# A two-layer hybrid attention step on one core: output products moved beside the last attention units, and three smaller moves

## The chip, the cores and the metric

The kernel runs on one NeuronCore of a Trainium2 chip. The metric is the device time of one execution in microseconds (us). A difference of 0.2%, about 2.8 us here, is about what a measurement of this kernel can tell from no change.

The engines are called as in the profile: PE is the matrix engine (PEld its weight loads), DVE the vector engine, ACT the scalar engine, POOL the general engine, SP the queue engine that issues most transfers. Each runs its own list of instructions in order; they are tied together by semaphores alone.

## What is computed

There are 384 tokens in three tiles of 128: tile 0 is the prompt, tiles 1 and 2 are the sample. The model width D is 2048. Two layers run one after the other.

```
x = x + gate * ((o * silu(g)) @ w_out)      per layer, o = attention over heads of width 128
layer 0: 8 heads of kind A (grouped query), 8 heads of kind B (neighbourhood, with a bias)
layer 1: 16 latent-attention heads; keys and values are made from a compressed state
y = rmsnorm(x) * final_norm                 after layer 1
```

In front of each layer stand a norm and a modulation; `q @ k`, softmax and `p @ v` are done per head and token tile. Prompt queries see 128 keys, sample queries 384.

## The kernel before, in words

**Weights and slots.** All weight matrices stream from HBM in pieces of 512 KB, the slots: two blocks of 128 rows by 512 columns. A chunk of 512 output columns takes eight slots (`SPC = 8`). Products are made in three matmuls from rounded parts: ACT copies the raw slot into `w_hi` (`split_hi`), DVE writes the remainder into `w_lo` (`split_lo`, L1176). Both are issued two slots ahead. The left operand is likewise held as `act_hi` and `act_lo`. `chunk_slot` on PE runs one slot for all three token tiles: 3 tiles x 2 blocks x 3 matmuls, into the banks `G[0..2]`.

**Attention units.** A unit is one head and one token tile. PE does four things for unit n: it turns its probabilities (`prob_turn`), computes the scores of unit n+2, does `attend` of unit n-1, and then runs one slot of some following product where `beside(n)` gives one. DVE does, per unit, `prob_copy`, `maximum` of unit n+2, `output` of unit n-1 (this writes the gated result into `u`), and then any `split_lo`. ACT does the exponentials. `attend` of a unit waits for `output` of the unit before it (`o_done`). Groups A0, A1 and B0 have 12 units each, with a product beside them. The last group of layer 0, B1 (12 units), and the last pair of heads of layer 1 (6 units) have none.

**Output product.** `turned_chunk` begins after the last `output`. It turns `u` block by block on PE (16 blocks of 128 columns, three transposes each, into the banks `BX`), ACT copies each into `act_hi`, DVE makes `act_lo`. Four blocks are turned ahead of the first slot, the others two behind each slot.

**Gates.** The last chunk before a group's units is its gate. ACT evacuates each gate tile twice (a half and a tanh, `evacuate_gate`): tile 0 ahead of the `split_hi` of the last slot, tiles 1 and 2 behind the exponential of unit 2. DVE finishes all three tiles at unit 1 (`finish_gate`, L1347).

**Queries of group A.** The four heads of a group are turned behind slots 4 to 7 of the gate chunk (`turn_in`), the first waiting for `qn_ready`, and DVE copies them into `qT`.

**Behind layer 0.** POOL waits for the last `output` and then loads gains, gate rows (through HBM, `gate_rows`), and the residual input. DVE's `residual(0)` (L1384, L1388) waits for these. The remainders of slots ten and eleven of the output product stand behind it on DVE.

**End.** After each tile's last residual, DVE sums squares, POOL takes the power, ACT scales the left half of the token's 2048 columns, DVE the right half, and SP stores two halves per tile (L386, L388). POOL waits for all stores (`y_out`) and leaves; a barrier of all engines ends the program (L168).

Of the kernel before, what the change touches and what calls it, by code (L numbers as in the profile page):

```python
# [54 lines left out]
N_A, N_B, N_OUT, N_GATE, N_H = 2, 2, D // CH, D // CH, 4  # L55
LAST = 3
Y_CUT = D // 2
# [108 lines left out]
def build(nc, t_in, t_out):  # L166
    ctx = ExitStack()
    with ctx:  # L168
# [160 lines left out]

        def evac_of(pair, c):  # L330

            return pair + ((0, None, 1, None, 2, 3, 4, 5)[c])
# [3 lines left out]
        def _(sp):  # L336
# [46 lines left out]
            for t in range(NT):  # L383
                out = t_out["y_prompt"][0] if t == 0 else t_out["y_sample"][0, (t - 1) * P:t * P, :]
                sp.wait_ge(y_left, t + 1)
                sp.dma_start(out[:, 0:Y_CUT], u[:, t, 0:Y_CUT]).then_inc(y_out, 16)  # L386
                sp.wait_ge(y_right, 2 * t + 2)
                sp.dma_start(out[:, Y_CUT:D], u[:, t, Y_CUT:D]).then_inc(y_out, 16)  # L388


        @block.tensor
        def _(pe):
# [17 lines left out]
            def chunk_slot(w, j, m, made=None, banks=G, depth=NT):  # L410
# [5 lines left out]
                for t in range(NT):  # L416
# [13 lines left out]
                last.then_inc(w_used, 1)  # L430
# [118 lines left out]
            def turn_out(x, parts, width=P, height=P):  # L549
                need(pe, x_free, x + 1 - len(BX))  # L550
                turn(BX[x % len(BX)], parts, width, height).then_inc(x_done, 1)
# [8 lines left out]
            def turned_chunk(x, w, m, made):  # L560

                for k in range(2 * KPS):
                    turn_out((x + k), token_blocks(u, k * P))
                for j in range(SPC):
                    chunk_slot((w + j), j, m, made)
                    for k in range(KPS * (j + 2), min(KPS * (j + 3), KT)):
                        turn_out((x + k), token_blocks(u, k * P))
# [67 lines left out]
            for i in range(N_A):  # L635
                m, tau, n0 = (M_A + i * (2 * NT)), (T_A + i * T_A_PER), (N_UA + i * UNITS)
                for j in range(SPC):
# [4 lines left out]
                    chunk_slot((W_A + j + i * (2 * SPC)), j, m)  # L642
# [26 lines left out]
            for i in range(N_B):  # L669
                w0, m = W_B + i * 4 * SPC, (M_B + i * 4 * NT)  # L670
                tau, n0 = (T_B + i * T_B_PER), (N_UB + i * UNITS)
                for j in range(3 * SPC):
                    if j == 3 * SPC - 1:
                        need(pe, t_free, tau + 2 * GROUP)
                        score(n0, 0, 0, 0)
# [8 lines left out]
                    if SPC + 1 <= j < SPC + 5:  # L684
# [4 lines left out]
                        turn_in(tau + (GROUP + h), [b[0], kcache[:, h * P:(h + 1) * P], b[1], b[2]])  # L689
                pe.wait_ge(vc_in, 16 * (i + 1))  # L690
# [6 lines left out]
                for n in range(UNITS):  # L697
# [5 lines left out]
                    for j in beside(n) if i < N_B - 1 else []:  # L703
                        chunk_slot((w0 + 3 * SPC + j), j, m + (3 * NT))
# [41 lines left out]
            def pair_product(g, c):  # L746
# [16 lines left out]
                bank_ = PAIR_BANKS[c % 4]  # L763
                if c < 4:
# [30 lines left out]
            def pair_attention(g, following):  # L795

                for n in range(PAIR_UNITS):
# [30 lines left out]
            pe.wait_ge(o_done, N_UH + N_H * UNITS)  # L828
            pe.wait_ge(t_free, T_H + N_H * T_H_PER)
            turned_chunk(X_U1, W_O1, M_O1, (x_free, X_U1))  # L830
# [7 lines left out]
        def _(act):  # L838
# [27 lines left out]
            def turned_high(x, out, width):  # L866

                need(act, x_done, x + 1)
                copy(out, BX[x % len(BX)][:, 0:width]).then_inc(xhi, 1)
# [80 lines left out]
            for i in range(N_A):  # L950
                m, tau, n0 = (M_A + i * (2 * NT)), (T_A + i * T_A_PER), (N_UA + i * UNITS)
                for j in range(SPC):
# [16 lines left out]
                    if j == SPC - 1:  # L969
                        exponent(n0, 0)  # L970
                        exponent(n0 + 1, 1)
                        need(act, qn_ready, (NT + i * NT))
                        evacuate_gate(m, w, i * CH, [0])
                    split_hi(w + 2)
                exponent(n0 + 2, 2)
                evacuate_gate(m, (W_A + SPC - 1 + i * (2 * SPC)), i * CH, [1, 2])
# [972 lines left out]
```

## Time and profile before

| | |
|---|---|
| time, median of 3 runs | 1412.71 us (1412.57 to 1413.67) |
| the profiled execution | 1412.55 us |
| its span, first to last instruction | 1410.8 us |
| mean granted PE clock | 0.995 of full |
| busy share | PE 96%, PEld 75%, DVE 43%, ACT 35%, POOL 4% |
| chain that ended last | PE 91%, DVE 4%, DMA 2%, issue 2%, ACT 1% |

The span lies 1.75 us under the execution's own time. A row of the timeline gives the start, the duration, the engine, the line, the operation, output and inputs, and in square brackets how long the engine was idle before it and what released it. Matmuls overlap: what one costs in a stream is the distance from start to start. A 32-bit score, transposition or `attend` is two passes, so "x2" can be one matmul of the code.

### The profile page before, as it was taken

The numbers are of one execution on the slowest core, as the hardware profiler recorded it, in microseconds if no ns is written. First come the engines' busy times: TensorE is split into PE (matmuls) and PEld (weight loads), VectorE is DVE, ScalarE is ACT, GpSimd is POOL, SyncE is SP. The second block draws the span as 40 slices with busy tenths as digits, with TensorE's granted clock in tenths as the row PEclk, the third lists the DMA queues.
The fourth block names the chain that finished last, engine by engine and source line by source line (L and its number), as shares of the span: only waits on it lengthen the run. The fifth ranks groups of instructions, "written<-read, shape, count | busy, mean of one in ns | idle before, by whom it ended". The sixth has DMA issues, their size and how long they took to land.

```text
span 1410.8 us, 17524 instructions
## 1 busy us (share of the span) xinstructions
PE 1359.5 (96%) x7011; PEld 1062.4 (75%) x7011; DVE 613.3 (43%) x1018; ACT 487.6 (35%) x806; POOL 61.6 (4%) x81
## 2 busy tenths in 40 slices
PE   6999999999999999999999899999999999999995
PEld 2567667677777777767888788888888998878884
DVE  3345644553332642236544532533434444445444
ACT  4234233232222322233334653333433333334332
POOL 3000000000100010001000100000000000010000
PEclk9999999999999999999999999999999999999998
DMA  9998767767767357743455343443322222134552
GB/s 370 395 404 337 279 209 246 276 232 260 285 246 252 115 197 236 255 153 131 151 189 176 117 131 114 134 133 120 120 75 63 73 75 75 60 124 154 161 159 90
DMA packets 70753, 260.14 MB, mean 184 GB/s; under 512 B 8584, under 2 KB 8712, under 8 KB 69392
## 3 DMA queue, kind: packets, MB, share of 16 engines
q1 hardware_dynamic: 64944, 237.58, 49.4%
q0 software_dynamic: 5584, 21.37, 4.5%
q8 instruction: 56, 0.92, 0.3%
q14 instruction: 25, 0.20, 0.0%
q10 hardware_dynamic: 144, 0.07, 0.0%
HBM read 251.05 MB, written 7.93 MB: 184 GB/s over the span
## 4 chain that ended last, share of the span: by engine, by line
PE 91%; DVE 4%; DMA 2%; issue 2%; ACT 1%; POOL 0%; SPq 0%; DVEq 0%; ACTq 0%
PE gemm L425 18%; PE gemm L427 18%; PE gemm L426 18%; PE ada_bank L499 4%; PE attended L593 3%; PE scores L575 3%; PE turned L545 3%; PE gemm L397 3%; PE gemm L399 3%; PE gemm L398 3%; PE ada_bank L521 2%; PE scores L578 2%; DMA ada<-in_ada_all 2%; PE ada_bank L399 1%; PE ada_bank L398 1%
## 5 line engine op out<-in xcount | busy, mean ns | idle before, releaser
L1176 DVE TENSOR_TENSOR w_lo<-w_raw,w_hi 128x1024 fp32r<-128x1024 f32 x246 | 303.7, 1240 | 480.7 <-ACT w_hi L839 480.4
L425 PE MATMUL gemm<-w_hi,act_lo 128*128 128x512 f32 x1146 | 457.4, 399 | 2.2 <-issue 1.4
L427 PE MATMUL gemm<-w_hi,act_hi 128*128 128x512 f32 x1146 | 447.1, 390 | 0.0
L426 PE MATMUL gemm<-w_lo,act_hi 128*128 128x512 f32 x1146 | 446.8, 390 | 0.0
L839 ACT ACTIVATE w_hi<-w_raw 128x1024 fp32r<-128x1024 f32 x246 | 258.1, 1057 | 404.5 <-PE gemm L427 340.1
L425 PEld LDWEIGHTS gemm<-w_hi,act_lo 128*128 128x128 f32 x1146 | 215.2, 188 | 62.7 <-issue 18.6
L427 PEld LDWEIGHTS gemm<-w_hi,act_hi 128*128 128x128 f32 x1146 | 215.1, 188 | 46.3
L426 PEld LDWEIGHTS gemm<-w_lo,act_hi 128*128 128x128 f32 x1146 | 215.5, 188 | 42.5
L895 ACT ACTIVATE prob<-scores,nmax 128x384 f32<-128x384 f32 (+1 forms) x96 | 49.1, 511 | 224.3 <-DVE nmax L1317 177.3
L1323 DVE COPY probT<-turned 128x384 f32<-128x384 f32 (+1 forms) x96 | 44.6, 465 | 59.3 <-PE turned L545 59.0
L575 PE MATMUL scores<-kT,qT 128*128 128x384 f32 (+1 forms) x192 | 63.8, 417 | 0.0
L593 PEld LDWEIGHTS attended<-v,probT 128*128 128x128 f32 x336 | 46.2, 191 | 21.2 <-issue 10.2
L499 PE MATMUL ada_bank<-ada,silu_c 128*32 128x512 f32 x512 | 61.6, 598 | 0.0
L593 PE MATMUL attended<-v,probT 128*128 128x128 f32 x336 | 50.3, 278 | 6.6 <-DVE u L1339 6.2
L521 PE MATMUL ada_bank<-ada,silu_c 128*32 128x512 f32 x256 | 39.7, 628 | 14.5 <-DMA ada<-in_ada_all 14.4
L1317 DVE TENSOR_REDUCE nmax<-scores 128x1 f32<-128x384 f32 (+1 forms) x96 | 44.4, 463 | 16.8 <-PE scores L578 13.6
L545 PE MATMUL turned<-ident,prob 128*128 128x128 f32 x224 | 40.8, 275 | 4.1 <-DVE probT L1323 2.0
L839 ACT ACTIVATE st<-gemm 128x512 f32<-128x512 f32 x36 | 21.5, 598 | 64.1 <-PE gemm L427 64.1
L545 PEld LDWEIGHTS turned<-ident,prob 128*128 128x128 f32 x224 | 27.9, 140 | 16.6 <-issue 12.3
L1339 DVE SCALAR_TENSOR_TENSOR u<-attended,rinv,u 128x128 f32<-128x128 f32 x96 | 33.7, 351 | 8.7 <-PE attended L593 3.2
L499 PEld LDWEIGHTS ada_bank<-ada,silu_c 128*32 128x32 f32 x512 | 13.4, 109 | 30.4 <-issue 30.4
L397 PE MATMUL gemm<-qn_hi,w_lo 128*128 128x384 f32 x96 | 33.8, 352 | 0.2 <-ACT st L888 0.2
(254 smaller groups left out, 1440.1 us busy)
## 6 DMA issues: line engine op xcount, KB each, us to landing
w_raw<-in_w_all SPq DMA_DIRECT2D x249, 512.0 KB, 3.6
ada<-in_ada_all SPq DMA_DIRECT2D x192, 512.0 KB, 7.5
gate_bc<-gate_scratch POOLq DMA_DIRECT2D x4, 1024.0 KB, 5.9
st<-x_scratch POOLq DMA_DIRECT2D x4, 768.0 KB, 4.9
x_scratch<-u POOLq DMA_DIRECT2D x3, 768.0 KB, 4.4
u<-in_x_sample SPq DMA_DIRECT2D x2, 1024.0 KB, 8.2
bias<-in_bias_all POOLq DMA_DIRECT2D x2, 1024.0 KB, 10.1
st<-in_x_sample POOLq DMA_DIRECT2D x4, 512.0 KB, 8.4
```

What stands on the lines that cost most here:

```text
L397: pe.matmul(out, alo, bhi, start=(n == 0), stop=False)
L398: pe.matmul(out, ahi, blo, start=False, stop=False)
L425: pe.matmul(bank_[:], alo, whi[:, kk], start=first, stop=False)
L426: pe.matmul(bank_[:], ahi, wlo[:, kk], start=False, stop=False)
L427: last = pe.matmul(bank_[:], ahi, whi[:, kk], start=False, stop=end)
L499: last = pe.matmul(AD[32 * g:32 * g + 32, :], silu_c[:, k, :], ada[:, r, gg * CH:(gg + 1) * CH], start=(k == 0), stop=(k == KT - 1), tile_ ...
L521: last = pe.matmul(AD[32 * g:32 * g + 32, :], silu_c[:, k, :], ada[:, at % ADA_RING, kk * CH:(kk + 1) * CH], start=(v == 0), stop=(v == 3) ...
L545: last = pe.transpose(bank_[0:width, n * height:(n + 1) * height], part, ident[0:height, 0:height])
L575: last = pe.matmul(s[:, 0:width], qT[:, h, t * P:(t + 1) * P], kT[:, kh, keys], start=True, stop=not latent)
L593: last = pe.matmul(out, probT[:, n % 2, b * P:(b + 1) * P], values(kt), start=(b == 0), stop=(b == len(tiles) - 1))
L839: copy = lambda out, in_, scale=1.0: act.activation(out, in_, ACT.Copy, scale=scale)
L1176: dve.tensor_tensor(w_lo[:, r, 0:width], w_raw[:, r, 0:width], hi_slot(w)[:, 0:width].bitcast(F32), ALU.subtract).then_inc(lo_ready, 1)
```

## The change

1. **Blocks turned early, layer 0.** The first 12 of the 16 blocks of `u` (`EARLY = 12`) belong to groups A0, A1 and B0. They are turned two at a time behind slots 16 to 21 of group B1, whose `act_hi` blocks have just been used.
2. **Blocks turned early, layer 1.** 12 blocks are turned one at a time in units 4 and 5 of pairs 1 to 6, into `G[0]` and `G[1]`. The next pair's first two products wait for the remainder of such a block.
3. **Output tiles beside units.** In B1 and in the last pair, each unit is followed by one token tile of a slot of the output product (`out_tile`, six matmuls). That places slots 0 to 3 in layer 0 and 0 and 1 in layer 1. `finish_turned_chunk` then runs one more slot, waits for the last `output`, turns the last four blocks and goes on.
4. **Splits.** `split_hi` for these slots stands at every third unit from unit 1 on, `split_lo` from unit 2 on.
5. **Gates.** ACT evacuates tiles 0 and 1 ahead of the exponential of unit 2 and behind `split_hi`, tile 2 behind it. DVE finishes one tile at each of units 1, 2 and 3.
6. **Queries of A.** Two heads are turned behind slots 5 and 6, the other two between the tiles of slot 7.
7. **End.** The middle token tile is scaled by ACT over 1536 columns, not 1024 (`Y_CUT`); `scale_right(0)` and `scale_left(0)` stand ahead of the next tile's work; SP waits for `y_out`, and POOL no longer does.

```
+EARLY = 12
-Y_CUT = D // 2
+Y_CUT = [D // 2, D - CH, D // 2]
+Y_RIGHT = [2, 3, 5]
...
+        def bank_of(x):
+            if X_U1 <= x < X_U1 + EARLY:
+                return G[(x - X_U1) % 2]
+            return BX[x % 4]
+        def early_u0(j):
+            k = 2 * (j - 2 * SPC)
+            return [k, k + 1] if 0 <= k < EARLY else []
+        def early_u1(g, n):
+            if 0 < g.index < 2 * N_H - 1 and n in (4, 5):
+                return [2 * (g.index - 1) + n - 4]
+            return []
...
SP
+            sp.wait_ge(y_out, 96)
...
PE
+            def out_tile(x, w, m, piece):
+                j = piece // NT
+                chunk_slot(w + j, j, m, (x_free, x), tiles=[piece % NT])
+            def finish_turned_chunk(x, w, m, first, o_all, t_all):
+                chunk_slot(w + first, first, m, (x_free, x))
+                pe.wait_ge(o_done, o_all)
+                pe.wait_ge(t_free, t_all)
+                for k in range(EARLY, KT):
+                    turn_out(x + k, token_blocks(u, k * P))
+                for j in range(first + 1, SPC):
+                    chunk_slot(w + j, j, m, (x_free, x))
...
+                        for t in range(NT):
+                            chunk_slot((W_A + j + i * (2 * SPC)), j, m, tiles=[t])
+                            if t < 2:
+                                turn_in(tau + (3 + t), token_blocks(stage[0], (2 + t) * P))
...
-                    if j >= 4:
-                        h = j - 4
-                        if h == 0:
-                            need(pe, qn_ready, (NT + i * NT))
-                        turn_in(tau + (1 + h), token_blocks(stage[0], h * P))
+                    if j in (5, 6):
+                        need(pe, qn_ready, (NT + i * NT))
+                        turn_in(tau + (j - 4), token_blocks(stage[0], (j - 5) * P))
...
+                    if i == N_B - 1 and early_u0(j):
+                        pe.wait_ge(o_done, n0)
+                        pe.wait_ge(t_free, tau + 2 * GROUP)
+                        for k in early_u0(j):
+                            turn_out(X_U0 + k, token_blocks(u, k * P))
...
+                    if i == N_B - 1:
+                        out_tile(X_U0, W_O0, M_O0, n)
...
-            pe.wait_ge(o_done, N_UH)
-            pe.wait_ge(t_free, T_H)
-            turned_chunk(X_U0, W_O0, M_O0, (x_free, X_U0))
+            finish_turned_chunk(X_U0, W_O0, M_O0, UNITS // NT, N_UH, T_H)
...
+                if c < 2 and g.index >= 3:
+                    pe.wait_ge(x_free, X_U1 + 2 * (g.index - 3) + c + 1)
...
+                    for k in early_u1(g, n):
+                        pe.wait_ge(o_done, g.n)
+                        pe.wait_ge(evac, evac_of(following.m, n) + 1)
+                        turn_out(X_U1 + k, token_blocks(u, k * P))
...
+                    if following is None:
+                        if n == 0:
+                            pe.wait_ge(x_free, X_U1 + EARLY)
+                        out_tile(X_U1, W_O1, M_O1, n)
...
ACT, group B (group A alike)
-                        evacuate_gate(m + (2 * NT), w, i * CH + N_A * CH, [0])
                     split_hi(w + 2)
+                    if i == N_B - 1:
+                        for k in early_u0(j):
+                            turned_high(X_U0 + k, act_hi[:, k, :], TOK)
+                evacuate_gate(m + (2 * NT), w, i * CH + N_A * CH, [0, 1])
                 exponent(n0 + 2, 2)
-                evacuate_gate(m + (2 * NT), w, i * CH + N_A * CH, [1, 2])
+                evacuate_gate(m + (2 * NT), w, i * CH + N_A * CH, [2])
...
+                    if i == N_B - 1 and n % NT == 1:
+                        split_hi(W_O0 + 2 + n // NT)
...
-            last_squares(N_OUT - 1, [0])
-            last_squares(N_OUT - 1, [1])
-            scale_left(0)
-            last_squares(N_OUT - 1, [2])
-            scale_left(1)
-            scale_left(2)
+            for t in range(NT):
+                last_squares(N_OUT - 1, [t])
+                scale_left(t)
...
DVE, group B
-                    if n == 1:
-                        finish_gate(m + (2 * NT), ((N_A + i) * NT), col)
+                    if 1 <= n <= NT:
+                        finish_gate(m + (2 * NT), ((N_A + i) * NT), col, [n - 1])
...
+                    if i == N_B - 1 and n % NT == 2:
+                        split_lo(W_O0 + 2 + n // NT)
...
+            scale_right(0)
             last_residual(1, M_END - NT, W_END)
             token_sum(1, SS_LAT + (N_OUT - 1) * NT)
-            scale_right(0)
...
POOL
-            pool.wait_ge(y_out, 96)
```

## Rows read from the trace of the kernel before

**Rows 1.** Page, part 1: busy time, share of the span, instructions.
```profile
PE 1359.5 (96%) x7011; PEld 1062.4 (75%) x7011; DVE 613.3 (43%) x1018; ACT 487.6 (35%) x806; POOL 61.6 (4%) x81
```

**Rows 2.** Timeline of PE in a slot of group B1, six matmuls apart.
```profile
584.03 0.39 PE L425 MATMUL gemm<-w_hi,act_lo 128*128 128x512 f32 x1
...
585.39 0.39 PE L425 MATMUL gemm<-w_hi,act_lo 128*128 128x512 f32 x1
```

**Rows 3.** Timeline of PE through the units of group B1.
```profile
628.63 0.27 PE L545 MATMUL turned<-ident,prob 128*128 128x128 f32 x1
...
630.32 0.39 PE L575 MATMUL scores<-kT,qT 128*128 128x128 f32 x2
630.54 0.39 PE L593 MATMUL attended<-v,probT 128*128 128x128 f32 x2
...
634.86 0.91 PE L593 MATMUL attended<-v,probT 128*128 128x128 f32 x6 [2.15 <-DVE u L1339]
...
638.76 0.52 PE L545 MATMUL turned<-ident,prob 128*128 128x128 f32 x3
639.11 0.81 PE L575 MATMUL scores<-kT,qT 128*128 128x384 f32 x2
639.76 0.83 PE L593 MATMUL attended<-v,probT 128*128 128x128 f32 x6
640.43 0.27 PE L545 MATMUL turned<-ident,prob 128*128 128x128 f32 x1
...
643.64 0.52 PE L545 MATMUL turned<-ident,prob 128*128 128x128 f32 x3
...
654.27 0.47 PE L425 MATMUL gemm<-w_hi,act_lo 128*128 128x512 f32 x1 [0.70 <-issue]
```

**Rows 4.** Timeline of PE in layer 1: last pair's first unit, output product's first matmul.
```profile
1243.62 0.27 PE L545 MATMUL turned<-ident,prob 128*128 128x128 f32 x1
...
1259.73 0.47 PE L425 MATMUL gemm<-w_hi,act_lo 128*128 128x512 f32 x1 [0.70 <-issue]
```

**Rows 5.** Timeline of PE around the starts of groups A0 and B0.
```profile
161.96 0.55 PE L545 MATMUL turned<-ident,st 128*128 128x128 f32 x3 [1.34 <-DVE st L1299]
...
181.44 0.30 PE L545 MATMUL turned<-ident,prob 128*128 128x128 f32 x1 [0.74 <-DVE qT L1323]
...
460.33 0.52 PE L545 MATMUL turned<-ident,prob 128*128 128x128 f32 x3 [0.42 <-DVE probT L1323]
```

**Rows 6.** Page, part 5: groups by line; busy us, mean ns, idle before.
```profile
L1176 DVE TENSOR_TENSOR w_lo<-w_raw,w_hi 128x1024 fp32r<-128x1024 f32 x246 | 303.7, 1240 | 480.7 <-ACT w_hi L839 480.4
...
L895 ACT ACTIVATE prob<-scores,nmax 128x384 f32<-128x384 f32 (+1 forms) x96 | 49.1, 511 | 224.3 <-DVE nmax L1317 177.3
```

**Rows 7.** Instructions on tile u: duration ns min/median/max, first and last start.
```profile
L1347 DVE SCALAR_TENSOR_TENSOR u<-st,u x24: 681/692/693, 183.6 to 1014.5; 128x512 f32<-128x512 f32 x24
```

**Rows 8.** Timeline of POOL and DVE behind layer 0's last unit.
```profile
652.29 0.55 POOL L1725 DMA_DIRECT2D gain_ql<-in_l_q_a_norm  x1 [61.86 <-DVE u L1339]
...
660.18 0.74 POOL L1808 DMA_DIRECT2D st<-in_x_sample  x1
...
694.53 1.90 DVE L1384 TENSOR_TENSOR st<-st,gate_bc 128x512 f32<-128x512 f32 x3
```

**Rows 9.** Landing of line 1808's transfers, 640 to 700 us.
```profile
DMA to landing us min/median/max: 8.1/9.8/11.5
```

**Rows 10.** Timeline of SP's queue at the end: stores of y.
```profile
1398.08 0.33 SPq L386 DMA_DIRECT2D out_y_sample<-u  x1
...
1399.40 0.33 SPq L386 DMA_DIRECT2D out_y_sample<-u  x1
```

**Rows 11.** Line 168, the closing barrier: duration ns min/median/max, first and last start.
```profile
L168 POOLq COMPARE_BRANCH  x1: 38/38/38, 1405.2 to 1405.2; - x1
L168 POOLq DRAIN  x1: 5209/5209/5209, 1405.3 to 1405.3; - x1
```

**Rows 12.** Windows: stretch, us, busy per engine, PEclk, DMA share, GB/s.
```profile
1400.00:1402.00 2.00, 0.00 (x0) 0.00 (x0) 0.00 (x0) 0.00 (x0) 0.00 (x0) 0.50 1.02 404
```

More of the change, by code:

```diff
@@ L408, in split_views, with chunk_slot @@
                         w_lo[:, w % RAW_RING, :].rearrange("p (k n) -> p k n", k=k))
-            def chunk_slot(w, j, m, made=None, banks=G, depth=NT):
+            def chunk_slot(w, j, m, made=None, banks=G, depth=NT, tiles=range(NT)):
                 need(pe, lo_ready, w + 1)
@@ L415, in chunk_slot @@
                 whi, wlo = split_views(w, KPS)
-                for t in range(NT):
+                for t in tiles:
                     if j == 0 and depth is not None:
@@ L868, in turned_high @@
                 need(act, x_done, x + 1)
-                copy(out, BX[x % len(BX)][:, 0:width]).then_inc(xhi, 1)
+                copy(out, bank_of(x)[:, 0:width]).then_inc(xhi, 1)
             def tile_done(m, w, t):
@@ L1023, in chunk_squares, with out_product @@
                         .then_inc(ss_ready, 1)
-            def out_product(x, xh, w, m, res, sums, chunks=N_OUT):
-                for k in range(2 * KPS):
+            def out_product(x, w, m, res, sums, chunks, first):
+                split_hi(w + first + 2)
+                for k in range(EARLY, KT):
                     turned_high((x + k), act_hi[:, k, :], TOK)
-                for j in range(SPC):
-                    for k in range(KPS * (j + 2), min(KPS * (j + 3), KT)):
-                        turned_high((x + k), act_hi[:, k, :], TOK)
+                for j in range(first + 1, SPC):
                     if j == SPC - 1:
@@ L1130, in pair_attention @@
                         exponent(g.n + (n + 2), (n + 2) % NT)
+                    for k in early_u1(g, n):
+                        turned_high(X_U1 + k, act_hi[:, k, :], TOK)
                     for c in range(8):
@@ L1133, in pair_attention @@
                             pair_out(following, c)
+                    if following is None and n % NT == 1:
+                        split_hi(W_O1 + 2 + n // NT)
             for c in range(8):
@@ L1152, in scale_left @@
                 act.wait_ge(gained, (N_OUT - 1) * NT)
-                copy(u[:, t, 0:Y_CUT], u[:, t, 0:Y_CUT], rstd[:, t:t + 1]).then_inc(y_left, 1)
+                part = u[:, t, 0:Y_CUT[t]]
+                copy(part, part, rstd[:, t:t + 1]).then_inc(y_left, 1)
             for j in range(SPC):
@@ L1341, in output, with finish_gate @@
                                          op0=ALU.mult, op1=ALU.mult).then_inc(o_done, 1)
-            def finish_gate(m, gates, col):
-                for t in range(NT):
+            def finish_gate(m, gates, col, tiles=range(NT)):
+                for t in tiles:
                     need(dve, evac, m + t + 1)
@@ L1348, in finish_gate, with low_block, finish_turned_chunk @@
                                              op0=ALU.add, op1=ALU.mult).then_inc(gate_done, 1)
-                need(dve, gate_done, gates + NT)
+                need(dve, gate_done, gates + tiles[-1] + 1)
             def turned_low(x, hi, out, width, high_at):
                 dve.wait_ge(xhi, high_at + 1)
-                dve.tensor_tensor(out, BX[x % 4][:, 0:width], hi.bitcast(F32), ALU.subtract)\
+                dve.tensor_tensor(out, bank_of(x)[:, 0:width], hi.bitcast(F32), ALU.subtract)\
                     .then_inc(x_free, 1)
-            def turned_chunk(x, xh, w):
-                for k in range(2 * KPS):
-                    turned_low(x + k, act_hi[:, k, :], act_lo[:, k, :], TOK, xh + k)
-                for j in range(SPC):
-                    for k in range(KPS * (j + 2), min(KPS * (j + 3), KT)):
-                        turned_low(x + k, act_hi[:, k, :], act_lo[:, k, :], TOK, xh + k)
+            def low_block(x, xh, k):
+                turned_low(x + k, act_hi[:, k, :], act_lo[:, k, :], TOK, xh + k)
+            def finish_turned_chunk(x, xh, w, first):
+                split_lo(w + first + 2)
+                for k in range(EARLY, KT):
+                    low_block(x, xh, k)
+                for j in range(first + 1, SPC):
                     split_lo(w + j + 2)
@@ L1508, in _ @@
                     split_lo(W_B + i * 4 * SPC + j + 2)
+                    if i == N_B - 1:
+                        for k in early_u0(j):
+                            low_block(X_U0, XH_U0, k)
                 for n in range(UNITS):
@@ L1647, in pair_attention @@
                         pair_output(g.before, PAIR_UNITS - 1)
+                    for k in early_u1(g, n):
+                        low_block(X_U1, XH_U1, k)
+                    if following is None and n % NT == 2:
+                        split_lo(W_O1 + 2 + n // NT)
                     for c in range(8):
```

67 lines of the change are left out of this document (33 added, 34 removed).

## The prediction

> **What bounds the kernel now.** I read the page first: PE is busy 96% of the span [rows 1]. That share counts overlapping matmuls and so hides short waits. I therefore took PE's timeline and measured from start to start. In a plain slot, six matmuls (one token tile) take 585.39 - 584.03 = 1.36 us, 0.227 each, without a hole [rows 2]. So a slot costs 4.08 us, and where only slots run nothing is to be won without fewer matmuls. The change removes none: its gain can only be waits of PE, and the end of the program.
>
> Four places have such waits. The first is group B1, where no product stands beside the units. From its first `prob_turn` to the first slot of the output product it is 654.27 - 628.63 = 25.6 us [rows 3]. PE's own work there follows from the same rows. A wide unit turns in 0.35 us (638.76 to 639.11), scores in 0.65, attends in 0.67. A narrow unit (prompt tile) needs 0.22 for the scores (630.32 to 630.54). Its other two steps I estimate at a third of the wide ones, 0.12 and 0.22. With 4 narrow and 8 wide units, two of whose scores are done before:
>
> - turns 4 x 0.12 + 8 x 0.35 = 3.3
> - ten scores 3 x 0.22 + 7 x 0.65 = 5.2
> - attends 4 x 0.22 + 8 x 0.67 = 6.2
> - four blocks of `u` ahead of the first slot 4 x 0.35 = 1.4
>
> That is 16.1 us of work in 25.6: **9.5 us of waits**. They come from the loop over DVE and ACT. Three units take 643.64 - 638.76 = 4.9 us where PE has 3.9 us of work. The longest single wait is 2.15 us, for the first `output`, which stands behind the three finished gate tiles [rows 3].
>
> The second place is the last pair of layer 1, built alike: 1259.73 - 1243.62 = 16.1 us [rows 4]. The work is 1.6 for turns (2 narrow, 4 wide), 4.3 for four scores (each twice the matmuls of layer 0), 3.8 for attends, 1.4 for blocks, together 11.1: **5.0 us of waits**.
>
> The third place is the start of the groups: PE idles 1.34 us for the normalised queries of A0, 0.74 us for the last head's copy in front of unit 0 (in A0, and the same again in A1, at 283.13), and 0.42 us for the first probability copy of B0 [rows 5].
>
> The fourth is the end: the stores of y and the closing barrier [rows 10 to 12].
>
> **The change, part by part.**
>
> *Tiles beside units, layer 0.* Each unit gets 1.36 us of matmuls. Three units then hold 3.9 + 4.1 = 8.0 us of PE work. The loop over DVE and ACT needs its 4.9 us plus one remainder of 1.24 us [rows 3, 6], 6.1. PE becomes the bound with 1.9 us to spare per three units. In the first units DVE has three gate tiles of 0.69 us in addition [rows 7]: 8.2 against 8.0. Following the queues, `output` of unit 2 comes behind gate tile 2 and the remainder of unit 2, and `attend` of unit 3 waits about 0.5 us. Otherwise I allow 0.6 us for hand-overs. Behind the last unit a whole slot (4.1 us) covers the last `output`, so that neither it nor the first blocks hold PE. Gain 9.5 - 1.1 = **8.4 us**.
>
> *Tiles beside units, layer 1.* Six tiles are 8.2 us of cover, and slot 2 covers the last `output`. I leave 0.5 us: gain **4.5 us**.
>
> *Blocks turned early.* Same number, same 0.35 us each, so no gain. In layer 0 they follow slots whose `act_hi` blocks are free. ACT's copy and DVE's subtraction cover 384 columns like an exponential of 0.51 us [rows 6], about 0.5 each. A slot of 4.08 us has room for two of each beside the split. In layer 1 the wait of the next pair's first two products for `x_free` is new. The chain turn, ACT, DVE is 0.5 + 0.5 and hand-overs, some 1.6 us (estimate). Behind the later of the two blocks one whole product of 24 half-wide matmuls still runs, by [rows 2] about 24 x 0.113 = 2.7 us. So it is hidden by 1.1 us. I charge 0.3 us for twelve single insertions: **-0.3 us**.
>
> *Starts of groups.* The queries of A are turned one slot later, which is 4 us of slack against 1.34. Heads 2 and 3 are turned between tiles, so that a tile of 1.36 us covers each copy. `split_hi` ahead of the gate evacuation brings the remainder, and the `prob_copy` behind it, earlier in B0. Evacuation of gate tile 2 waits for the exponential of unit 2 as before. Gain 1.34 + 2 x 0.74 + 0.42 = **3.2 us**; at worst 0, if other waits take their place.
>
> *Behind layer 0.* POOL's loads start at the last `output` (652.29) and the residual input is issued at 660.18 and lands 11.5 us later, at 671.7, 19.4 us behind the start [rows 8, 9]. `residual(0)` ran at 694.53, so the loads had 23 us to spare. Now only slots 4 to 7 remain behind the last `output`: 4 x 4.08 + 1.4 - 0.6 = 17.1 us, then 3.4 us to the residual as before (chunk end 654.27 + 8 x 4.08 + 12 x 0.35 = 691.1, residual 694.53). That is 20.5 us against 19.4: nearly all of the slack is gone. If the landing comes late, DVE stands in `residual(0)` with the remainder of slot ten behind it. That remainder had 0.7 us to spare: it was ready at 694.53 + 3.8 + 1.2 = 699.5, and PE needed it at 691.1 + 0.9 (two blocks of modulation rows) + 8.2 = 700.2. I cost this at nothing. Each microsecond of landing beyond 1.8 costs one.
>
> *The end.* POOL passes its wait for y at 1405.2 and only then begins a DRAIN of 5.2 us, after which the barrier falls at 1410.8 [rows 11]. With the wait on SP, POOL begins its DRAIN behind its last power, at about 1398.2, and is through by 1403.4. The stores now decide. Before, 2.1 MB were issued from 1398.08 on and moved at 404 GB/s [rows 10, 12], 5.2 us, leaving 1405.2 - 1403.3 = 1.9 us of latency. Now the middle token's left 0.79 MB leave by about 1396.3, under the last tile's work, and its right part of 0.26 MB ahead of the last token. What is issued at 1399.40 is 1.05 MB, 2.6 us: landed at 1399.4 + 2.6 + 1.9 = 1403.9, and 0.3 us for the barrier gives 1404.2. Gain 1410.8 - 1404.2 = 6.6, of which 1.3 come from the stores and 5.3 from the DRAIN; I take **6.5 us**. The bounds are 0 (neither moves) and 7.4 (POOL alone decides).
>
> A rule speaks against this. The Trainium skill, VectorE: DVE Perf Modes, section "The DRAIN you can't avoid", has the DRAINs around a kernel at about 12 ns, constant on all engines. By it a DRAIN costs nothing of its own, and moving the wait would bring the stores' 1.3 us alone. The row of 5209 ns does not agree with it.
>
> **Sum**, against the profiled execution's 1412.55 us (0.16 under the median of 1412.71): 8.4 + 4.5 - 0.3 + 3.2 + 6.5 = 22.3, so **1390.3 us**.
>
> **The rivals.**
>
> *The DRAIN follows the stores (0.12).* Its 5.2 us are no work of its own but time that POOL needs after the last traffic, wherever the wait stands. For it: no row says what the DRAIN waits for. Against it: all transfers had landed and all other engines were through when it began, so there was nothing left to wait for. Then only 1.3 us come from the end: 1390.3 + 5.2 = 1395.5. The section of the Trainium skill named above would give this time too.
>
> *DVE becomes the bound in the units (0.14).* `finish_gate`, remainders and `output` share one queue. If hand-overs make a round of three units 1.9 us longer than 6.1, PE waits again. Half of 9.5 + 5.0 would stay, some 7 us against the 1.6 that I left: 1390.3 + 5.5 = 1395.8. For it: 8.2 against 8.0 in the first units. Against it: later rounds have 1.9 us to spare.
>
> *The residual input is late (0.04).* A landing 4 us later than 671.7's equivalent costs 2.2 us: 1392.5. It stands inside the likeliest range.
>
> *Slower (0.03).* The early blocks are not hidden. If PE, at each of the 24, waits out the chain of 1.6 us over ACT and DVE (through `x_free` or the banks), that costs 38 us: 1390.3 + 38 = 1428. It decides from 22.3 / 24 = 0.93 us a block. Against it: a block's buffer is asked for four blocks later in layer 0, and a whole product later in layer 1.
>
> *No change (0.02).* The waits reappear one for one in the slots behind, because DVE's remainders set the pace there: 1412. Against it: PE's slots run without a hole at present [rows 2].
>
> **How the numbers follow.** The forecast has 0.65, and its own range is 1387.5 to 1393.5: the end's 7.4 and leftover waits of 0 on one side, group starts at 1 and a late residual input on the other. The range to hold 8 in 10 takes in both rivals near 1395.7 and reaches from 1387.0 to 1397.0. What can be told from no change is 0.2%, 2.8 us. All cases but the last two lie beyond it on the fast side: faster 0.95, same 0.02, slower 0.03.
>
> **What the changed profile would show.** In B1 `gemm` matmuls between units, about 2.7 us a unit, and no wait for `u` L1339 over 0.6 us; from the first `prob_turn` to the first matmul of slot 4 about 16.1 - 1.4 + 16.3 + 1.1 = 32.1 us. In layer 1 turned blocks with no idle time in front of the products behind them. No idle PE at the start of A0, A1 and B0. POOL's DRAIN starting near its last power and still 5.2 us long, and the span ending less than 1 us behind the last landing. Wrong would be: a DRAIN behind the landing, waits for `probT` or `u` in each unit, or `w_lo` awaited behind `residual(0)`.

## The result, and the profile after

The changed kernel takes **1389.35 us**, median of 4 runs (1388.98 to 1389.77), against 1413.09 us (1412.57 to 1413.67) for the kernel before, run beside it. The ratio is 0.9832, 95% interval 0.9815 to 0.9849. The profiled execution took 1389.77 us with a span of 1387.9 us, 22.8 us under the profiled execution before (1412.55). One of the six executions of the experiment with the stores as before took 2286 us at a granted clock of 0.56; it is left out of that experiment's median.

The page's first part of the changed kernel answers to [rows 1]: as many matmuls, 6.8 us less of PE's busy time, and DVE and ACT unchanged.

```profile
PE 1352.7 (97%) x7011; PEld 1061.8 (77%) x7011; DVE 613.3 (44%) x1017; ACT 487.5 (35%) x806; POOL 61.7 (4%) x81
```

**Where the time went.** I followed the same landmarks in both timelines of PE. The table says by how much PE is ahead at each. Twelve blocks are turned earlier in the changed kernel. They cost about 0.33 us each, 3.93 us in all, wherever they stand, and that is taken out.

| landmark | before | after | ahead |
|---|---|---|---|
| first `prob_turn` of B1 (12 blocks already done after) | 628.63 | 629.53 | 3.03 |
| modulation rows turned behind the output product's first chunk | 691.17 | 679.05 | 12.12 |
| first `prob_turn` of the last pair (12 blocks of layer 1 done after) | 1243.62 | 1236.05 | 11.50 |
| last matmul | 1394.41 | 1377.77 | 16.64 |
| end of the span | 1410.8 | 1387.9 | 22.9 |

So: starts of groups 3.0, units of B1 9.1, behind layer 0 a loss of 0.6, the last pair and what follows it 5.1, the end 6.2.

PE's timeline in B1 after the change (start, duration, engine, line, what, idle before and its releaser) answers to [rows 3]:

```profile
639.67 0.49 PE L567 MATMUL turned<-ident,prob 128*128 128x128 f32 x3
640.00 0.39 PE L603 MATMUL scores<-kT,qT 128*128 128x128 f32 x2
640.80 0.46 PE L621 MATMUL attended<-v,probT 128*128 128x128 f32 x2 [0.41 <-DVE u L1392]
641.01 0.47 PE L446 MATMUL gemm<-w_hi,act_lo 128*128 128x512 f32 x1
...
642.25 0.39 PE L448 MATMUL gemm<-w_hi,act_hi 128*128 128x512 f32 x1
642.48 0.49 PE L567 MATMUL turned<-ident,prob 128*128 128x128 f32 x3
642.81 0.81 PE L603 MATMUL scores<-kT,qT 128*128 128x384 f32 x2
643.46 0.83 PE L621 MATMUL attended<-v,probT 128*128 128x128 f32 x6
...
645.51 0.27 PE L567 MATMUL turned<-ident,prob 128*128 128x128 f32 x1
```

Six `gemm` matmuls stand between the steps of two units, and in all of B1 the 0.41 us for the output of unit 2 is the only wait of PE that shows, where there had been waits up to 2.15 us. Behind the units, slot 4 starts at 661.25, 31.7 us after the first `prob_turn`.

The same order of gate tiles stands in the other three groups, where it brings waits that were not there before, or lengthens one:

```profile
178.95 0.33 PE L567 MATMUL turned<-ident,prob 128*128 128x128 f32 x1
...
195.35 0.46 PE L621 MATMUL attended<-kT,probT 128*128 128x128 f32 x2 [0.70 <-DVE u L1392]
...
471.07 0.35 PE L621 MATMUL attended<-v,probT 128*128 128x128 f32 x1 [1.17 <-DVE u L1392]
```

The first line is the start of unit 0 in A0, without the 0.74 us of [rows 5]. The other two are `attend` of unit 3 in A0 and B0. A1 has the same 0.70 at 296.46, and B0 had 0.45 there before.

Behind layer 0, the timelines of POOL, DVE and PE answer to [rows 8]:

```profile
671.21 0.74 POOL L1874 DMA_DIRECT2D st<-in_x_sample  x1
...
683.64 1.90 DVE L1439 TENSOR_TENSOR st<-st,gate_bc 128x512 f32<-128x512 f32 x3 [1.26 <-DMA st<-in_x_sample]
...
688.66 0.50 PE L446 MATMUL gemm<-w_hi,act_lo 128*128 128x512 f32 x1 [0.40 <-DVE w_lo L1229]
```

The residual input lands 12.3 us after its issue. DVE stands 1.26 us in front of `residual(0)`, and the remainder behind it comes late for PE: matmul starts show a hole of 0.55 us there. In the profiled execution of the repeat, the same kernel's input landed after 11.3 us, DVE waited 0.50 us and PE not at all. So the 0.6 us belong to this one execution.

The end: POOL's last power, SP's last stores and the closing barrier (the lines of L170 have the duration in ns as min/median/max, and the start), for [rows 10, 11]:

```profile
1380.83 0.99 POOL L1788 TENSOR_TENSOR rstd<-ms,mhalf 128x1 f32<-128x1 f32 x1 [3.21 <-DVE ms L1317]
```
```profile
1383.02 0.33 SPq L406 DMA_DIRECT2D out_y_sample<-u  x1
1383.40 0.43 SPq L408 DMA_DIRECT2D out_y_sample<-u  x1
```
```profile
L170 POOLq DRAIN  x1: 5836/5836/5836, 1381.2 to 1381.2; - x1
...
L170 SPq COMPARE_BRANCH  x1: 38/38/38, 1387.5 to 1387.5; - x1
```

POOL's DRAIN is issued while the last power still runs, which is why it reads 5.84 us. It ends at 1387.05, that is 5.23 us behind the end of the power. The stores have landed when SP passes at 1387.51, and the span ends 0.4 us later. POOL alone would have allowed an end 0.46 us earlier, no more.

### The profile page after: what moved, and what is told of

Same layout as the page of the kernel before. It is cut to its first block, busy times and chain, and to the rows that moved or that the text cites. A ratio compares the mean times of both kernels' runs of the same rounds, so it can differ in the third digit from the quotient of the medians.

```text
span 1387.9 us, 17569 instructions
## 1 busy us (share of the span) xinstructions
PE 1352.7 (97%) x7011; PEld 1061.8 (77%) x7011; DVE 613.3 (44%) x1017; ACT 487.5 (35%) x806; POOL 61.7 (4%) x81
## 4 chain that ended last, share of the span: by engine, by line
PE 92%; DMA 3%; DVE 2%; issue 1%; POOL 1%; ACT 1%; SPq 0%; DVEq 0%; ACTq 0%; POOLq 0%
PE gemm L446 18%; PE gemm L448 18%; PE gemm L447 18%; PE ada_bank L521 4%; PE attended L621 3%; PE scores L603 3%; PE gemm L418 3%; PE gemm L420 3%; PE gemm L419 3%; PE turned L567 3%; PE ada_bank L543 2%; PE scores L606 2%; DMA ada<-in_ada_all 2%; PE ada_bank L419 1%; PE ada_bank L420 1%
## 5 line engine op out<-in xcount | busy, mean ns | idle before, releaser
L1370 DVE TENSOR_REDUCE nmax<-scores 128x1 f32<-128x384 f32 (+1 forms) x96 | 44.4, 463 | 15.5 <-PE scores L606 12.3
L521 PEld LDWEIGHTS ada_bank<-ada,silu_c 128*32 128x32 f32 x512 | 13.4, 109 | 30.4 <-issue 30.4
L543 PEld LDWEIGHTS ada_bank<-ada,silu_c 128*32 128x32 f32 x256 | 7.6, 110 | 35.5 <-issue 21.9
```

The source lines that it names most:

```text
L521: last = pe.matmul(AD[32 * g:32 * g + 32, :], silu_c[:, k, :], ada[:, r, gg * CH:(gg + 1) * CH], start=(k == 0), stop=(k == KT - 1), tile_ ...
L543: last = pe.matmul(AD[32 * g:32 * g + 32, :], silu_c[:, k, :], ada[:, at % ADA_RING, kk * CH:(kk + 1) * CH], start=(v == 0), stop=(v == 3) ...
```

## The experiments

Each ran beside the kernel before on the same chip. Ratios are to that kernel, with 95% intervals, and differences are to the changed kernel's 1389.35 (1389.40 in the repeat below). A difference between two experiments below about 2.8 us is not told by the times alone, so there the traces carry the reading. Beside the last three experiments the changed kernel ran again:

> The changed kernel unaltered, for comparison within this call: 1389.4 us, by every theory.

1389.40 us (1388.82 to 1389.69), ratio 0.9823 [0.981, 0.9837].

### The closing barrier

**POOL waits for y again.**

```
-            sp.wait_ge(y_out, 96)
...
             for t in range(NT):
                 token_power(POW_Y, t)
+            pool.wait_ge(y_out, 96)
```

> The changed kernel with one thing undone: POOL waits for y again, SP does not. Theory (POOL's closing DRAIN is work of its own of 5 to 6 us, which starts when POOL is through with its waits): POOL passes the wait at about 1387.5, where SP passed it, the DRAIN of 5.2 to 5.8 us stands behind it, and the span grows by 5.2 to 5.8 us: about 1394.9 us against 1389.35. Rival A (the DRAIN's length depends on where it stands, and behind the stores it is short because nothing is left on POOL's queue): less than 1 us slower, 1389.4 to 1390.3. Rival B (the 6.2 us of the end came from the stores' split): no difference.

**The kernel before with the wait moved, and nothing else.**

```
+            sp.wait_ge(y_out, 96)
...
-            pool.wait_ge(y_out, 96)
```

> The kernel before with one thing of the change: SP waits for y, POOL does not. Theory: the DRAIN starts behind the last power at about 1398.3 and ends at 1403.5 to 1404.1, beside the stores; SP passes its wait at 1405.15 and the span ends 0.4 us behind it, 1405.5 instead of 1410.8: 5.2 us faster, about 1407.7 us. Rival A (the DRAIN follows the last traffic): it ends 5 us behind the landing wherever the wait stands, no difference to before. Rival B (most of the end's 6.2 us came from the stores): 1 to 2 us faster only.

Measured with POOL waiting in the changed kernel: 1394.48 us (1393.96 to 1394.81), ratio 0.9866 [0.9854, 0.9879], 5.1 us slower than the changed kernel. The kernel before with the wait moved took 1408.74 us (1407.33 to 1409.32), ratio 0.9966 [0.9954, 0.9978], 4.7 us faster than 1413.40 beside it; the spans of the profiled executions differ by 5.3. The barrier's lines, first of the one where POOL waits:

```profile
L170 POOLq COMPARE_BRANCH  x1: 41/41/41, 1386.6 to 1386.6; - x1
L170 POOLq DRAIN  x1: 5213/5213/5213, 1386.7 to 1386.7; - x1
```

and of the kernel before with SP waiting:

```profile
L168 POOLq DRAIN  x1: 5566/5566/5566, 1397.8 to 1397.8; - x1
L168 SPq COMPARE_BRANCH  x1: 38/38/38, 1405.1 to 1405.1; - x1
```

Alone behind everything the DRAIN lasts 5.21 us, as in [rows 11]. Beside the stores it ends 5.24 us behind the power (1397.40 + 0.72 to 1403.36). So the DRAIN neither follows the traffic nor shrinks in another place. From the start of the last power to the end of the span it is 13.3 us before, 8.1 with the wait moved, and 7.1 in the changed kernel, which leaves 1.0 for the stores.

**The stores as before** (`Y_CUT` and the order of scaling undone, SP waits).

```
-Y_CUT = [D // 2, D - CH, D // 2]
-Y_RIGHT = [2, 3, 5]
+Y_CUT = [D // 2, D // 2, D // 2]
+Y_RIGHT = [2, 4, 6]
...
-            scale_right(0)
             last_residual(1, M_END - NT, W_END)
             token_sum(1, SS_LAT + (N_OUT - 1) * NT)
+            scale_right(0)
```

> The changed kernel with the stores of y cut and ordered as before (half and half for each token tile, scaling of a tile behind the sum of the next), the wait on SP kept. Theory of the prediction's term: the last stores carry 2.1 MB instead of 1.05 MB and land 1.3 us later, 1.0 to 1.3 us slower, 1390.3 to 1390.7 us. Rival (the landing is bound by its latency, not by its bytes): less than 0.4 us slower.

Measured: 1390.06 us (1389.83 to 1390.64), ratio 0.9836 [0.9824, 0.9849], 0.7 us slower, which the times alone don't tell from nothing. In the trace the last stores left at 1382.47, and SP passed at 1387.83, 7.67 us behind the start of the last power against 6.68. That is 1.0 us, over the rival's 0.4. The term holds, a little under its 1.3.

### Tiles beside the units

**Layer 0 without them**: the twelve blocks stay early, all slots of the product and their splits stand behind the units.

```
-                    if i == N_B - 1:
-                        out_tile(X_U0, W_O0, M_O0, n)
...
-            finish_turned_chunk(X_U0, W_O0, M_O0, UNITS // NT, N_UH, T_H)
+            finish_turned_chunk(X_U0, W_O0, M_O0, -1, N_UH, T_H)
```

> The changed kernel without tiles of the output product beside the units of group B1: its twelve blocks are still turned early, and all eight slots of the output product stand behind the units. Theory (the tiles fill PE's waits in B1): the units take their 25.6 - 1.4 us again without cover, and 8.4 to 9.1 us come back, less the 0.55 us that the late residual input costs now (it has its 23 us to spare again): 1397.2 to 1398.2 us. Rival (the early blocks, not the tiles, brought it: ahead of the first slot PE no longer waits for the chain of turn, copy and subtraction): 0 to 3 us slower, up to 1392.4.

**Layer 1 without them**, in the same way.

> The same for layer 1: no tiles of the output product beside the six units of the last pair, the twelve blocks still turned early. Theory: 4.5 to 5.1 us come back, 1393.9 to 1394.5 us. Rival (the early blocks brought part of it, or the units had no waits worth filling): 0 to 2.5 us slower.

Layer 0: 1396.48 us (1396.04 to 1397.0), ratio 0.9879 [0.9865, 0.9892], 7.1 us slower. Between B1's first `prob_turn` and the modulation rows PE takes 686.93 - 628.96 = 57.97 us instead of 49.52. The tiles alone are thus worth 8.45 us there, and the other 0.6 of the 9.1 came from what this experiment keeps: the order of the gate tiles and the early blocks. The profiled executions differ by 7.2 and not 8.45, because the late residual input (0.55) is in time again and this execution was 0.5 us ahead before A0's units. The time lies below the theory's range (1397.2), and the rival's 0 to 3 us is refuted. Two of the waits that the tiles cover:

```profile
635.51 0.35 PE L622 MATMUL attended<-v,probT 128*128 128x128 f32 x1 [0.92 <-DVE u L1390]
...
637.82 0.46 PE L622 MATMUL attended<-v,probT 128*128 128x128 f32 x1 [0.86 <-DVE u L1390]
```

Layer 1: 1393.27 us (1392.94 to 1393.56), ratio 0.9856 [0.9842, 0.9869], 3.9 us slower. PE takes from the last pair's first `prob_turn` to the last matmul 145.63 us instead of 141.72, again 3.9 and not the theory's 4.5 to 5.1. The kernel before took 150.79, of which 3.93 are its twelve blocks. So 1.2 us of layer 1's 5.1 came without tiles, as the rival had it in part. The first slot no longer stands behind four blocks that were turned just before, and the 0.70 us wait of [rows 4] is gone; where the other 0.5 lay is not shown.

### The starts of the groups

**Queries of A turned as before**, one head behind each of slots 4 to 7.

```
-                    if j in (5, 6):
-                        need(pe, qn_ready, (NT + i * NT))
-                        turn_in(tau + (j - 4), token_blocks(stage[0], (j - 5) * P))
+                    if j >= 4:
+                        h = j - 4
+                        if h == 0:
+                            need(pe, qn_ready, (NT + i * NT))
+                        turn_in(tau + (1 + h), token_blocks(stage[0], h * P))
```

> The changed kernel with the queries of groups A0 and A1 turned as before: one head behind each of slots 4 to 7, head 3's copy by DVE ahead of unit 0, no turn between the tiles. Theory (the waits of 1.34 us in A0 and of 0.74 us in each group were the price of that order): 2.5 to 2.8 us slower, 1391.9 to 1392.1 us, with idle time ahead of the first turned queries of A0 and ahead of unit 0 in both. Rival (evacuation and finishing of single gate tiles brought the gain of the groups' starts): less than 1 us slower.

(DVE's copies alike.) Measured: 1392.59 us (1392.44 to 1392.73), ratio 0.9851 [0.9838, 0.9865], 3.2 us slower, where the three waits make 2.8: the order of the queries also closed some 0.4 us of shorter holes. The waits of [rows 5] are back to the hundredth, at 162.05, 181.53 and 283.51:

```profile
162.05 0.44 PE L567 MATMUL turned<-ident,st 128*128 128x128 f32 x2 [1.34 <-DVE st L1349]
...
181.53 0.30 PE L567 MATMUL turned<-ident,prob 128*128 128x128 f32 x1 [0.74 <-DVE qT L1373]
...
283.51 0.30 PE L567 MATMUL turned<-ident,prob 128*128 128x128 f32 x1 [0.74 <-DVE qT L1373]
```

**Each gate tile finished one unit earlier.** Why does `attend` of unit 3 wait? DVE's timeline in the changed kernel, A0:

```profile
188.29 1.23 DVE L1229 TENSOR_TENSOR w_lo<-w_raw,w_hi 128x1024 fp32r<-128x1024 f32 x1 [0.63 <-ACT w_hi L886]
192.89 0.29 DVE L1376 COPY probT<-turned 128x128 f32<-128x128 f32 x1 [3.38 <-PE turned L567]
193.47 0.56 DVE L1370 TENSOR_REDUCE nmax<-scores 128x1 f32<-128x384 f32 x1 [0.29 <-PE scores L603]
193.94 0.68 DVE L1400 SCALAR_TENSOR_TENSOR u<-st,u 128x512 f32<-128x512 f32 x1
194.66 0.16 DVE L1388 RECIPROCAL rinv<-rsum 128x1 f32<-128x1 f32 x1
194.85 0.35 DVE L1392 SCALAR_TENSOR_TENSOR u<-attended,rinv,u 128x128 f32<-128x128 f32 x1
```

Gate tile 2 (L1400) stands in unit 3, directly ahead of the output that PE asks for, and just before it DVE was idle for 3.38 us.

```
-                    if 1 <= n <= NT:
-                        finish_gate(m, (0 + i * NT), i * CH, [n - 1])
+                    if n < NT:
+                        finish_gate(m, (0 + i * NT), i * CH, [n])
```

(and alike in group B)

> The changed kernel with each gate tile finished one unit earlier (tile n in unit n instead of n + 1), in all four groups of layer 0. Theory (the new waits of attend for the output of unit 2, 0.70 in A0, 0.70 in A1, 1.17 in B0 and 0.41 in B1, are the 0.68 us of gate tile 2 on DVE ahead of that output, where DVE had been idle for 3.4 us in the unit before): the waits fall to 0 in A0 and A1, to 0.5 in B0, to 0 in B1, 2.0 to 2.5 us faster, about 1387.1 us. Rival A (the wait moves to an earlier unit, whose probability copy or output stands behind the tile now): 0 to 0.5 us faster. Rival B (in B1 DVE has too little room in the first units): up to 1 us slower there.

Measured: 1386.56 us (1386.21 to 1386.86), ratio 0.9808 [0.9795, 0.9822], **2.8 us faster** than the changed kernel, more than expected. In A0 the same step now follows without a wait:

```profile
194.17 0.39 PE L603 MATMUL scores<-kT,qT 128*128 128x128 f32 x2
194.62 0.46 PE L621 MATMUL attended<-kT,probT 128*128 128x128 f32 x2
```

A1 and B1 likewise, and B0 is back at its 0.45. That is 0.70 + 0.70 + 0.72 + 0.41 = 2.5, which is shown. The 0.55 us behind `residual(0)` is gone too, but this is not shown to be the edit's work: the input landed 11.7 us after its issue here, and in the changed kernel's own repeat (11.3 us) the hole is absent as well.

### Behind layer 0

**The first residual input issued early.**

```
+            pool.wait_ge(gate_done, (N_A + N_B) * NT)
+            residual_in(0)
             pool.wait_ge(o_done, N_UH)
```

(`residual_in` holds the two loads, and the loop starts with chunk 1)

> The changed kernel with POOL's two loads of the first residual input of layer 0 issued as soon as the last gate tile is finished, ahead of its wait for the last output, instead of behind the gains and gate rows. Theory (the late landing of that input held DVE by 1.26 us and through the remainder behind it PE by 0.55 us): residual(0) of layer 0 starts 1.0 to 1.3 us earlier, the 0.40 us wait for w_lo near 688.7 is gone, 0.4 to 0.55 us faster, about 1388.9 us. Rival (the broadcast of the gate rows, issued only 1.6 us ahead of that input, is as late): residual(0) moves by less than 0.5 us and the time by 0 to 0.2 us.

Measured: 1389.08 us (1388.84 to 1389.52), ratio 0.9829 [0.9816, 0.9841], 0.3 us faster, which the times alone don't tell from nothing. In its trace `residual(0)` starts at 682.10, behind the `mod` instructions and without a wait, and PE does not wait for `w_lo` there. So the theory's mechanism holds; what it is worth varies from one execution to the next, since the unaltered kernel's repeat has no wait of PE there either.

**Both repairs together.**

> The changed kernel with both repairs: each gate tile finished a unit earlier, and the first residual input of layer 0 loaded as soon as the last gate tile is finished. With the earlier gate tiles alone the landing of that input already held DVE by only 0.48 us and PE not at all. Theory: the two overlap, 0 to 0.3 us faster than the earlier gate tiles alone (1386.6), 1386.3 to 1386.6 us. Rival (the sum of both single gains, 2.8 + 0.3): 1386.2 us or less; the two can't be told apart by time alone, the wait of residual(0) in the trace tells: 0.

Measured: 1386.65 us (1386.22 to 1386.93), ratio 0.9805 [0.9792, 0.9818]. It is no faster than the earlier gate tiles alone. In its trace `residual(0)` starts without a wait (679.42).

### How much room DVE has between the units

**One or two more subtractions** on DVE ahead of each remainder in B1 (into a buffer that is unused there).

```
                     if i == N_B - 1 and n % NT == 2:
+                        w = W_O0 + 2 + n // NT
+                        need(dve, hi_ready, w + 1)
+                        for _ in range(1):        # or 2
+                            own.add(dve.tensor_tensor(stage_flat[:, 0:SLOT], w_raw[:, w % RAW_RING, :],
+                                                      hi_slot(w).bitcast(F32), ALU.subtract))
+                            own.sync()
```

> The changed kernel with one more subtraction of 1.22 us on DVE (into an unused buffer) ahead of the remainder in units 2, 5, 8 and 11 of group B1. Theory (PE is the bound there: a round of three units lasts 8.0 us and DVE is busy for 5.8 of them, the prediction gave it 1.9 us to spare): 0 to 0.3 us slower, 1389.4 to 1389.7. Rival (DVE sets the pace between units, since each probability copy must be through before the next attend): each of the rounds is 0.8 to 1.2 us longer, 3 to 4.5 us slower in all.

> The same with two more subtractions, 2.45 us, ahead of the remainder in units 2, 5, 8 and 11 of group B1. Theory (1.9 us to spare by the prediction, 2.2 by the busy times): 0.3 to 0.6 us over in each of three to four rounds, 1 to 2.4 us slower, 1390.4 to 1391.8. Rival (a queue that must answer within one unit of 2.7 us has less room than the round's sum says): 1.5 to 2.4 us over in each, 4.5 us slower or more.

Measured: 1392.25 us (1391.94 to 1393.22), ratio 0.9845 [0.9832, 0.9859], 2.9 us slower; and 1400.83 us (1400.48 to 1403.17), ratio 0.9908 [0.9895, 0.9922], 11.4 us slower. Both are far over the theory; the first is just under the rival's bound, the second over it. The waits of PE with one more:

```profile
641.65 0.46 PE L621 MATMUL attended<-v,probT 128*128 128x128 f32 x2 [1.37 <-DVE u L1392]
...
650.11 0.46 PE L621 MATMUL attended<-v,probT 128*128 128x128 f32 x2 [0.22 <-DVE u L1392]
...
658.58 0.35 PE L621 MATMUL attended<-v,probT 128*128 128x128 f32 x1 [0.45 <-DVE u L1392]
```

The listed waits leave out the short holes, so I measured rounds of three units on PE, from the first `prob_turn` of one to the first of the next (the last one to slot 4):

| units | changed kernel | one more | two more |
|---|---|---|---|
| 3 to 5 | 8.66 | 9.92 | 12.77 |
| 6 to 8 | 8.00 | 8.46 | 9.72 |
| 9 to 11 | 7.74 | 8.41 | 9.67 |

```profile
646.36 0.27 PE L567 MATMUL turned<-ident,prob 128*128 128x128 f32 x1
...
654.82 0.27 PE L567 MATMUL turned<-ident,prob 128*128 128x128 f32 x1
...
663.23 0.48 PE L446 MATMUL gemm<-w_hi,act_lo 128*128 128x512 f32 x1
```

(The lines are of the one with one more.) From start to start the added instruction takes 1.25 us of DVE. In units 3 to 5 it costs 1.26 us, so there is no room at all, beside the gate tile and the 0.41 us wait that stands there already. In the next two rounds it costs 0.46 and 0.67 us, which leaves 0.8 and 0.6 us of room. Two more (2.5 us) cost 1.72 and 1.93 us in the same two rounds: again a room of 0.8 and 0.6. So DVE is busy for 5.9 of 8.0 us in the round of units 6 to 8, but the room is 0.8 us and not 2.1. In the trace, the remainders delay the probability copy and the output of the next unit, and it is these that PE waits for; spare time later in the round does not help.

The rounds make 2.4 of the 2.9 us with one more and 7.8 of the 11.4 with two. Most of the rest lies behind the units. The added instructions of unit 11 stand ahead of the last `output`, for which POOL's loads wait. With two more, DVE waits 2.72 us for the residual input, and PE then 1.82 us for the remainder behind it.

With two more, PE also lost time in a way that is no wait. Windows (stretch, its length, busy time per engine, granted clock, DMA share, GB/s):

```profile
638.00:642.00 4.00, 2.45 (x14) 1.68 (x13) 3.90 (x7) 0.10 (x1) 0.00 (x0) 1.00 0.36 120
642.00:646.00 4.00, 2.81 (x8) 2.19 (x9) 2.06 (x7) 1.98 (x5) 0.00 (x0) 0.69 0.00 0
646.00:650.00 4.00, 4.00 (x21) 3.26 (x20) 2.85 (x6) 0.67 (x2) 0.00 (x0) 0.89 0.00 0
694.00:698.00 4.00, 2.18 (x10) 1.52 (x9) 3.97 (x7) 1.06 (x1) 1.13 (x2) 1.00 0.40 127
698.00:702.00 4.00, 4.00 (x12) 3.10 (x12) 1.98 (x2) 0.00 (x0) 0.84 (x2) 0.57 0.99 337
702.00:706.00 4.00, 4.00 (x19) 3.31 (x18) 1.07 (x1) 1.06 (x1) 0.00 (x0) 1.00 0.66 206
```
```profile
699.35 0.63 PE L447 MATMUL gemm<-w_lo,act_hi 128*128 128x512 f32 x1
699.77 0.63 PE L448 MATMUL gemm<-w_hi,act_hi 128*128 128x512 f32 x1
700.20 0.63 PE L446 MATMUL gemm<-w_hi,act_lo 128*128 128x512 f32 x1
...
701.74 0.39 PE L447 MATMUL gemm<-w_lo,act_hi 128*128 128x512 f32 x1
701.97 0.40 PE L448 MATMUL gemm<-w_hi,act_hi 128*128 128x512 f32 x1
```

Behind two waits of 1.37 us (they end at 641.08 and 643.20), and again behind a single one of 1.82 us (697.76), the granted clock fell to the lower level (1.2 GHz). Matmuls then start 0.43 us apart and not 0.227, until about 646.7 and 701.5, and that costs another 1.6 us each time. This is why units 3 to 5 lose 4.1 us to 2.5 us of added work.

## Why the prediction was right, and where its terms were off

The forecast was 1390.3 us, and 1389.35 lies in the likeliest case's own range. Against the profiled execution the sum was 22.3, and 22.8 were measured. The places and mechanisms of the gain were right. That the sum fits to 0.5 us is partly luck: single terms were off by up to 0.7 us either way and largely cancelled.

- **Tiles in layer 0, 8.4.** Measured 9.1 in the changed kernel's trace; the tiles alone give 8.45, so 0.6 came from other parts of the change. The 0.5 us expected at `attend` of unit 3 is the 0.41 us wait. The 32.1 us to slot 4 came as 31.7.
- **Tiles in layer 1, 4.5.** Measured 5.1: 3.9 from the tiles and 1.2 without them. The working counted all 5.0 us of waits as the tiles' to fill. One of these waits goes with the early blocks instead.
- **Early blocks, -0.3.** Over the pairs of layer 1, PE's lead falls from 11.44 us (1036.06 before, 1024.62 after) to 7.57 at the last pair's start. That is 3.87 us for twelve blocks, against 3.93 of bare work: insertion cost nothing, and PE has no listed wait in layer 1's pairs. The rival that ends slower is refuted by that.
- **Starts of groups, 3.2.** Measured 3.0 at the start of B1, but not as worked out. The four waits went as priced, and undoing the queries' order brought the three of group A back exactly. The step that failed is "No idle PE at the start": finishing the gates one at a time put tile 2 ahead of the output of unit 2. I had followed that queue in B1, found 0.5 us there, and did not do it for A0, A1 and B0. They wait 0.70, 0.70 and 1.17 us now (B0 0.45 before). That is 2.1 us of new waits. Shorter holes that the change closed elsewhere in the groups, none over 0.35 us and 1.9 us in all, made up for them. The working had none of these holes, so that this term came out right by luck. Some 0.4 us of them go with the queries' order; which edit closed the others was not tested.
- **Behind layer 0, nothing.** The mechanism was right and the size was off. I had the landing 11.5 us after the issue and 1.1 us to spare; it took 12.3, and output to issue took 9.0 us instead of 7.9, since POOL waited 4.53 us for the gate rows' way through memory (3.45 before). The price was 0.55 us, by the "late residual" rival's mechanism, in this execution and none in the repeat.
- **The end, 6.5.** Measured 6.2: 5.2 for the DRAIN and 1.0 for the stores, predicted 5.3 and 1.3. Its rival (the DRAIN follows the stores) is refuted by both experiments with the wait. The Trainium skill, VectorE: DVE Perf Modes, section "The DRAIN you can't avoid", puts the DRAINs of a kernel's preamble and postamble at about 12 ns on every engine. SP's closing DRAIN is near it (7 ns behind its wait, 123 ns in the kernel before), and POOL's 5.2 us in every run of this case is not. The page ascribes its DRAINs to the runtime, while those here stand at a line of the kernel (L168, L170). So it may not speak of them at all; the prediction took them for the same DRAINs.
- **DVE as the bound.** The rival did not come about, but its threshold was closer than I wrote: "1.9 us to spare" per round of three units was nothing in units 3 to 5 and 0.8 and 0.6 us in the next two rounds. 1.25 us more of DVE work per round takes back 2.9 us, and 2.5 us more takes back 11.4. The chance of 0.14 was not too high.

## What to carry to other kernels

When a queue of short answers (copy, output) is filled with other work, sum the work for each unit and not for each round: an engine that is busy for 5.9 of 8.0 us had 0.8 us of room. After an order of instructions is changed in one stage, follow the queue by hand in every stage that shares the code; here that found 2.8 us. And wait for the last stores on an engine whose closing DRAIN is short, so that POOL's 5.2 us run beside them.

## What the runs showed of the hardware

- POOL's closing DRAIN ends about 5.2 us (5.21 to 5.24 where both ends were read to the hundredth) after POOL's last work or wait in every profiled execution, whether stores are in flight or nothing is. The record reads up to 5.84 us where it was issued beside a running power.
- Two waits of 1.37 us close behind each other, and elsewhere a single one of 1.82 us, were each followed by a granted clock of 1.2 GHz, at a price of 1.6 us each. The kernel before had a wait of 2.15 us in the same group of units, and its granted clock stayed at 1.00 there, so the length of one wait does not decide it. What does was not tested.
- The landing of one small input (0.5 MB) took 12.3 us from its issue in one execution of the changed kernel and 11.3 in another. PE lost 0.55 us in the first and nothing in the second, because the slack there was used up.
